# Third block of a hybrid decoder step: value tiles among the first group's level steps, last query tiles behind them, weight units in that order, narrower masked copies

## What is computed

```python
def _mixer_c(h, hg_s, lower_bound, w_in, hg_gn, w_out):
    ...
    qp, fp, ip, gp = _split(jnp.einsum('bld,de->ble', h, w_in), C_SPLITS)
    f = lower_bound + (1.0 - lower_bound) * jax.nn.sigmoid(fp.astype(f32))
    ...
    q = jax.nn.silu(qp.astype(f32)).reshape(shp)
    k = (1.0 - f).reshape(shp)
    log_f = jnp.log(f).reshape(shp)
    v = ip.astype(f32).reshape(B, L, HG_HEADS, HG_DV)
    o, s_new = _hgrn2(q, k, log_f, v, hg_s.astype(f32))
    ...
```

## Times and profile before

| | us |
|---|---|
| median of 3 runs | 1539.3 |
| lowest and highest run | 1535.43, 1540.26 |
| profiled execution | 1531.38 |
| its span | 1529.6 |
| PE busy in the span | 1497.9 |
| DVE busy | 1170.9 |
| ACT busy | 913.5 |

### The profile page before, as it was taken

How to read it: one execution, slowest core, us unless ns; L and a number is a source line. 1 busy time by engine, 2 the same in 40 slices (tenths; PEclk the granted TensorE clock), 3 DMA queues, 4 the chain that set the end, 5 groups by cost and what they waited for, 6 DMA issues and landing times.

```text
span 1529.6 us, 23416 instructions
## 1 busy us (share of the span) xinstructions
PE 1497.9 (98%) x8701; PEld 1326.0 (87%) x8701; DVE 1170.9 (77%) x1286; ACT 913.5 (60%) x909; POOL 89.5 (6%) x95
## 2 busy tenths in 40 slices
PE   9999999999999989999999999999999999999997
PEld 8899889999999979989778888888888888888885
DVE  5756687555555897767698888988889888898986
ACT  5444645334334553245677777878777787776863
POOL 1023110000000000120300000000000000000003
PEclk9999999999999999999999999999999999999999
DMA  8577625996456423442899999999999999999993
GB/s 243 138 135 145 120 87 149 314 294 179 123 152 206 131 65 99 129 148 67 323 393 363 382 360 401 390 364 386 360 398 377 380 386 362 388 378 384 391 351 119
DMA packets 213588, 403.87 MB, mean 264 GB/s; under 512 B 13471, under 2 KB 130491, under 8 KB 213390
## 3 DMA queue, kind: packets, MB, share of 16 engines
q1 hardware_dynamic: 203120, 372.82, 70.2%
q0 software_dynamic: 6320, 22.20, 4.9%
q10 hardware_dynamic: 4078, 7.89, 1.4%
HBM read 372.58 MB, written 30.28 MB: 263 GB/s over the span
## 4 chain that ended last, share of the span: by engine, by line
PE 89%; DVE 9%; issue 1%; ACT 1%; DVEq 0%; POOL 0%; ACTq 0%; POOLq 0%
PE bank L488 26%; PE bank L489 26%; PE bank L490 26%; DVE dense_lo L1756 2%; PE bank L706 2%; PE bank L1109 1%; PE bank L963 1%; PE bank L748 1%; PE bank L630 1%; PE bank L651 1%; DVE w_lo L2286 1%; PE bank L698 1%; DVE arena L2129 0%; DVE arena L2108 0%; PE bank L639 0%
## 5 line engine op out<-in xcount | busy, mean ns | idle before, releaser
L2286 DVE TENSOR_TENSOR w_lo<-arena,w_hi 128x2048 fp32r<-128x2048 f32 (+1 forms) x280 | 597.3, 2167 | 86.2 <-ACT w_hi L1635 84.9
L1635 ACT ACTIVATE w_hi<-arena 128x2048 fp32r<-128x2048 f32 (+1 forms) x280 | 500.7, 1820 | 114.2 <-PE bank L490 113.2
L488 PE MATMUL bank<-w_hi,xg_hi 128*128 128x512 f32 (+1 forms) x768 | 288.2, 375 | 2.8 <-DVE w_lo L2286 2.3
L489 PE MATMUL bank<-w_lo,xg_hi 128*128 128x512 f32 (+1 forms) x768 | 286.7, 373 | 0.0
L490 PE MATMUL bank<-w_hi,xg_lo 128*128 128x512 f32 (+1 forms) x768 | 285.8, 372 | 0.0
L1756 DVE TENSOR_TENSOR dense_lo<-ring,dense_hi 128x2048 fp32r<-128x2048 f32 (+1 forms) x78 | 167.9, 2153 | 122.6 <-ACT dense_hi L1311 122.6
L1311 ACT ACTIVATE dense_hi<-ring 128x2048 fp32r<-128x2048 f32 (+1 forms) x78 | 140.5, 1803 | 161.1 <-PE bank L490 127.4
L488 PEld LDWEIGHTS bank<-w_hi,xg_hi 128*128 128x128 f32 x768 | 144.9, 189 | 32.0 <-issue 3.6
L490 PEld LDWEIGHTS bank<-w_hi,xg_lo 128*128 128x128 f32 x768 | 144.6, 188 | 26.1
L489 PEld LDWEIGHTS bank<-w_lo,xg_hi 128*128 128x128 f32 x768 | 144.9, 189 | 25.0
L488 PE MATMUL bank<-h_hi,dense_hi 128*128 128x320 f32 x448 | 142.3, 318 | 4.0 <-DVE h_lo_a L1769 1.4
(11 more groups left out here) (431 smaller groups left out, 2401.5 us busy)
## 6 DMA issues: line engine op xcount, KB each, us to landing
arena<-in_w_moe_down SPq DMA_DIRECT2D x176, 512.0 KB, 6.5
arena<-in_w_moe_gate SPq DMA_DIRECT2D x128, 512.0 KB, 6.6
arena<-in_w_moe_up SPq DMA_DIRECT2D x128, 512.0 KB, 6.8
arena<-in_w_moe_gate SPq DMA_DIRECT2D x64, 384.0 KB, 5.4
arena<-in_w_moe_up SPq DMA_DIRECT2D x64, 384.0 KB, 4.1
ring<-in_w_in_ab SPq DMA_DIRECT2D x32, 512.0 KB, 9.7
ring<-in_w_in_c SPq DMA_DIRECT2D x32, 512.0 KB, 4.5
expert_rows<-ZERO SPq DMA_DIRECT2D x12, 1024.0 KB, 8.0
```

What stands on the lines that cost most here:

```text
L488: mm(out, left[0], right[0], start=start, stop=False)
L489: mm(out, left[0], right[1], start=False, stop=False)
L1635: fn(WH[SLOT_OF[p]][:, 0:unit_size(p)], STAGE[:, s, 0:unit_size(p)], ACT.Copy).then_inc(S("unit_hi"), 1)
L2286: v.tensor_tensor(WL[w][:, 0:n], STAGE[:, s, 0:n], WH[w][:, 0:n].bitcast(F32), ALU.subtract).then_inc(S("unit_split"), 1)
```

## The change

Three edits. The list `C_STEPS` gets another order in its first five lines: `rt`, v0 and v1 stand behind the query tile q3, v2 behind `pa1`, v3, v4 and v5 between the later levels of group a, and the query tiles q4 to q7 are moved behind them, q4 and q5 around `scan1` and q6 and q7 around `end0`. The forget tiles f4 to f7 move back by two to four steps. `C_ORDER` names single units now, with the order that fits the list: the value units of heads 0 to 3 stand fifth and eighth, those of query heads 4 to 7 ninth and tenth. Last, the masked copies take only the later half of each block of a level, 128 columns in place of 256.

```diff
-    f0 wh wl wh ms f1 forget0 f2 wh f3 ln0 wl forget1 forget2 forget3 q0 q1 wh wl scan0 q2 q3 f4 xa0 da1 f5 xa1
+    f0 wh wl wh ms f1 forget0 f2 wh f3 ln0 wl forget1 forget2 forget3 q0 q1 wh wl scan0 q2 q3 rt v0 xa0 da1 v1 xa1
...
-        C_ORDER = [2, 0, 3, 1, 4, 5, 6, 7]
+        C_ORDER = [(2, 0), (2, 1), (0, 0), (0, 1), (4, 0), (3, 0), (3, 1), (4, 1), (1, 0), (1, 1),
+                   (5, 0), (5, 1), (6, 0), (6, 1), (7, 0), (7, 1)]
...
-                mask = level[:, j, :].bitcast(mybir.dt.uint32).unsqueeze(1).to_broadcast([P, 2, P])
+                m = 1 << j
+                later = lambda x: x.rearrange("p i (n m) -> p i n m", m=2 * m)[:, :, :, m:2 * m]
+                mask = level[:, j, :].bitcast(mybir.dt.uint32).rearrange("p (n m) -> p n m", m=2 * m)[:, :, m:2 * m]
+                mask = mask.unsqueeze(1).to_broadcast([P, 2, P // (2 * m), m])
...
-                        ins = v.copy_predicated(both, mask, b[:, 2 * q * P:2 * (q + 1) * P].rearrange("p (i n) -> p i n", n=P))
+                        src = b[:, 2 * q * P:2 * (q + 1) * P].rearrange("p (i n) -> p i n", n=P)
+                        ins = v.copy_predicated(later(both), mask, later(src))
```

More of the change, by code:

```diff
@@ L69 @@
 C_STEPS = [(w.rstrip("0123456789"), int("0" + w.lstrip("abcdefghijklmnopqrstuvwxyz_"))) for w in """
-    f0 wh wl wh ms f1 forget0 f2 wh f3 ln0 wl forget1 forget2 forget3 q0 q1 wh wl scan0 q2 q3 f4 xa0 da1 f5 xa1
[L71 to L74, removed]
+    f0 wh wl wh ms f1 forget0 f2 wh f3 ln0 wl forget1 forget2 forget3 q0 q1 wh wl scan0 q2 q3 rt v0 xa0 da1 v1 xa1
+    pa0 wh wl la0 da2 la1 pa1 v2 xa2 wl da3 pa2 xa3 f4 la2 f5 wh pa3 da4 wl f6 da5 xa4 la3 f7 la4 xa5 pa4 forget4 da6
+    v3 forget5 sig1 pa5 forget6 la5 v4 xa6 la6 wh pa6 v5 forget7 ln1 wl da7 q4 scan1 xa7 q5 wh la7 pa7 wl q6 end0
+    xend0 kend0 q7 silu1 wh xb0 wl v6 pb0 db1 xb1 wh lb0 turn0 lb1 v7 la8 wl db2 pb1 xb2 v8 out0 pb2
+    lb2 db3 state0 turn1 xb3 lb3 sq0 wh pb3 out1 wl v9 turn2 db4 out2 sq1 db5 xb4 lb4 state1 v10 state2
     pb4 db6 xb5 g0 lb5 turn3 sq2 xb6 wh v11 pb5 out3 wh wl pb6 sq3 lb6 wl g1 db7 xb7 g2 pb7 g3 lb7 end1 state3
@@ L391, in trunk_kernel @@
         WIDE = (0, 1, 2)
-        C_ORDER = [2, 0, 3, 1, 4, 5, 6, 7]
+        C_ORDER = [(2, 0), (2, 1), (0, 0), (0, 1), (4, 0), (3, 0), (3, 1), (4, 1), (1, 0), (1, 1),
+                   (5, 0), (5, 1), (6, 0), (6, 1), (7, 0), (7, 1)]
         plan = [(kind, c, half) for kind, order in (("ab", AB_ORDER), ("oab", range(2)), ("ffn", range(NFC)),
-                                                    ("fd", range(KD)), ("c", C_ORDER), ("oc", range(2)))
+                                                    ("fd", range(KD)))
                 for c in order for half in range(2)]
+        plan += [("c", *unit) for unit in C_ORDER] + [("oc", c, half) for c in range(2) for half in range(2)]
         NDENSE = len(plan)
```

## The result

The changed kernel has a median of 1548.97 us (1544.76 to 1559.84, 10 runs) against 1533.72 us (1529.94 to 1540.26, 10 runs) for the kernel before on the same chip. The ratio is 1.0104, with a 95% interval from 1.0084 to 1.0125: the change costs 16 us (13 to 19). The forecast was a cost of 13.4 us and a time of 1552.7; the base of that time, the median of three runs, was 5.6 us above the median of ten, and the cost was too low by 1.9 us (the two medians lie 15.3 apart) or 2.6 (by the ratio). The two errors have opposite signs, so that the time came out only 3.7 us too high is in part luck.

The account below looks back on a forecast made before the run. DVE was taken to bound PE in group a's last part. Idle 15.2 + 3.2 − 8.4 = +10.0 and clock +3.4 made +13.4 us on a median of 1539.3: 1552.7, range 1543 to 1559.5.

Parts of the forecast that it names:

- What bounds it: Last part of group a: DVE is the bound; PE's waits there cost 8.4 us plus 1.7 of clock, 10.1 to win.
- The three floors: Behind v5, la7 and q7, PE waits for low parts before q4, q6 and v6: 3.4, 4.1, 7.7 us, sum 15.2.
- The third chain: Behind q7, from q6's end to v6: 11.3 us of DVE and ACT steps, 3.6 covered by q7, leaving 7.7 idle.
- The level steps: Waits at la1, la5 and la6 in group a: 3.2 us taken, bounds nothing and 6.4.
- DVE's stall at da4: da4 waits for la3, now behind f4, la2, f5 and f6: DVE idles about 3 us and starts pa4 late.
- The clock: Falls behind all three low-part waits at 1.7 us each: 5.1 us, 3.4 more than before.
- The narrower copies: Save about 0.10 us of DVE each, 2.8 a group; costed at nothing on PE's path; in group b DVE waits for PE.
- From v9 on every start later by a constant.: From v9 on the order is as before, so every PE start is later by one constant, 13 us or so.
- The fillers work: Value tiles cover every wait and no new one comes: 1529.2 us; decided by the split's place at v5's copy; chance 0.05.
- Only the floors: No level waits and no clock falls, only the three low-part waits: +5.1 us, 1544.4; chance 0.12.
- Group b is short of cover: Six of group b's twelve value tiles moved ahead, so three more level waits, 6.4 us: 1559.1; chance 0.13.

Follow-up runs that it names:

- the control with the old order: The kernel before, its product order kept, with narrower copies, v0's low part made earlier and silu1 ahead of la7, pa7 and end0: 1529.88 us, ratio 0.9988.
- the repaired kernel: The changed kernel with ninth to eleventh units' splits earlier, la3's copies ahead of da5, silu1 and q7 ahead of end0: 1524.59 us, ratio 0.9939.
- the early splits: The changed kernel with the high and low parts of the ninth, tenth and eleventh units each made earlier: 1534.74 us, ratio 0.9986.
- the idle matmuls: The changed kernel with 24, 32 and 60 matmuls whose result nobody reads put into its three low-part waits: 1543.47 us, ratio 1.0054.
- the swapped high part: The changed kernel with the eleventh unit's high part ahead of silu1 on ACT instead of behind it: 1544.84 us, ratio 1.0084.
- the one early split: The changed kernel with only the ninth unit's high and low parts made before the copies of la6 and pa6: 1542.93 us, ratio 1.0060.
- the wide-copy run: The changed kernel's new order with the masked copies back at their old width: 1550.41 us, ratio 1.0117.
- the narrow-copy one: The kernel before, in its old order, with only the narrower masked copies: 1530.96 us, ratio 0.9981.

## Why the prediction was right, point by point

- **What bounds it.** Right: DVE's queue sets PE's waits in group a, and the delay is carried to the end; the stage's +16.2 is the ratio's +16.
- **The three floors.** Right in place, cause and size: 3.4, 4.1 and 7.7 us forecast, 3.56, 4.40 and 7.83 measured. They were 0.6 us longer in sum than forecast. Moving the low parts ahead took them away, all three or one alone, and the time followed.
- **The third chain.** Right term by term: from q6's copy (598.25) to v6 (609.56) it takes 11.3 us, as forecast. What I had not seen is that 3.2 us of it, silu1 and the high part, hung on one position in ACT's queue.
- **The level steps.** 3.2 us forecast, 4.3 measured (2.15 + 1.36 + 0.82), inside the bounds. But the largest piece is not one that I named. I had asked of every tile which DVE step its *operands* wait for, and not when the *bank* it writes comes free: v3 needs a bank of the ring of five, and la3's copies, which free it, stood behind da5, itself waiting for PE's la4. The level waits that I did name, of la1, la5 and la6, come to 2.2 us in the changed kernel and to 3.5 (0.82 + 1.18 + 1.47) once v3's wait is gone, near the 3.2; that v3's wait stood in for one of them is luck.
- **DVE's stall at da4.** About 3 us forecast, 2.75 measured. da5's 1.41 behind it was the start of v3's wait, and I had not followed it on.
- **The clock.** It fell behind all three waits, as forecast, but the term was too small: 6.4 − 1.7 = +4.7 us, forecast +3.4. The one fall of before, with its 1.7 us, was at the low end of the four seen (1.65 to 2.5). This term (1.3), the level term (1.1) and the floors (0.6), less the 0.2 that I had missed in the old waits, are 2.8 us; the cost was too low by 2.8 in the stage and 2.6 by the ratio. "TensorE: Matmul & The Clock Gate", section "What's actually happening", in the Trainium skill has activity release the clock, so that a pause is paid twice; the run with unread matmuls in the pauses bears it out, as they won 4.8 us with the low parts no earlier than before. Not every pause was paid so: the last section has waits behind which the clock held.
- **The narrower copies.** Right that they are hardly on PE's path in group a in either order as it stood (stage −0.1 and −0.5 us), and silent on the order once repaired, where they bring 1.3. Wrong for group b, where DVE was said to wait for PE: in all three pairs of traces the wide copies leave PE a wait of 0.5 to 0.7 us for the products of one level (line 963 or 965, 0.47, 0.68 and 0.58 us), and the narrow ones at most 0.3. It is too small to change the forecast. The size was 0.13 us a copy from start to start (0.09 in the mean of the recorded lengths, 439 to 345 ns), except in the last two levels (below). The estimate of 0.13 that the prediction worked out from "VectorE: DVE Perf Modes", section on the TRN2 errata, in the Trainium skill agrees with it.
- **"From v9 on every start later by a constant."** Nearly: from the second step of the state to the router the changed kernel's trace takes 114.3 us against 111.5. The difference is about that of one wait of 3.0 us for the transfer of the old state (`in_state_hgrn`) before an output. That wait turns up in the runs of five kernels with 1.4 to 3.0 us, among them the control with the old order, and is missing in others; so it does not go with the new order alone.
- **The rivals.** "The fillers work" was a true possibility at its one point, where the splits stand: with the splits ahead of the copies and nothing else moved, the loss is gone (ratio 0.9986), and with the bank's and silu1's waits taken away too the kernel is 0.6% faster. Its price was −10.1 us, the repaired kernel has −9. "Only the floors" failed on the clock. "Group b is short of cover" did not occur: the changed kernel's trace has no wait of 0.5 us or more for its levels. The 6.1 us that I set against this rival were of both groups; 5.2 of them are group b's (3.02 us ahead of 620.20 and 2.14 ahead of 631.87), which leaves the argument as it was.

## What to carry to other kernels

Moving filler work in front of waits helps only if what the *next* tile needs stands in front of the fillers' own clean-up on the engine that makes it. When an order is rewritten, ask for each tile on the bottleneck engine three things: what its operands wait for, when the bank that it writes comes free, and what the releasing engine does just before, table loads and its own waits included. A loss that sits in a few such places can be taken away by moving the releasing steps alone. Here that only brought the kernel back to where it was; the fillers paid once the waits beneath, for a bank and for silu1, were moved as well.

## What the chip did that I had not expected

Whether the clock falls does not follow from the length of the wait alone. v3's wait of 2.15 us stands in five traces; behind it the clock held in two (the changed kernel and the early splits) and fell in three (the idle matmuls, the swapped high part, the one early split), with 2.94 and 4.4 us for the same tile. In the wide-copy run it held after 2.43 us, in the narrow-copy one it fell after 2.50. And in the run with the swapped high part, which had lost the clock at v3, the wait of 3.56 us before q4 cost nothing: q4 ran at full speed. The cost of a fall was 1.65, 2.5 and 2.2 us behind waits of 3.56, 4.40 and 7.83 us. The slow phases themselves do grow, to about 3, 7 and 10 us by the windows of 2 us, but the cost does not grow in step, because behind the longest wait half of the slow phase is over before PE starts:

```profile
604.00:606.00 2.00, 0.00 (x0) 0.00 (x0) 0.08 (x1) 1.89 (x2) 0.00 (x0) 0.58 0.00 0
606.00:608.00 2.00, 0.00 (x0) 0.00 (x0) 0.79 (x1) 1.98 (x2) 0.00 (x0) 0.50 0.00 0
608.00:610.00 2.00, 0.44 (x2) 0.44 (x3) 1.50 (x1) 1.54 (x2) 0.00 (x0) 0.50 0.00 0
```

The clock was already down for the last 5 us of v6's wait, while behind the wait of 3.56 us it fell only after q4 had begun.

A masked copy whose runs are one or two elements long saves less. Four copies of the seventh level, where the runs have two elements, in the changed kernel:

```profile
586.68 1.29 DVE L2135 COPY_PREDICATED arena<-cst,bank 128x128 f32<-128x128 uint32 x4
587.76 0.48 DVE L2140 COPY_PREDICATED arena<-cst,bank 64x256 f32<-64x256 uint32 x1
```

From start to start they take 1.08 us, 0.27 each. Those of the last level, neighbouring tokens with runs of one, take 1.11 us in the run with the narrower copies alone, where nothing holds them up:

```profile
584.09 1.31 DVE L2133 COPY_PREDICATED arena<-cst,bank 128x128 f32<-128x128 uint32 x4
585.20 0.49 DVE L2138 COPY_PREDICATED arena<-cst,bank 64x256 f32<-64x256 uint32 x1
```

The same copies of the other levels take 0.79, 0.20 each, and the old ones of 256 columns 0.33 in every level. The prediction had looked for this in a group of additions and seen no sign.
